# A fused two-block kernel on Trainium2: the late chunks of w_ada summed by one-column products

## What the kernel computes

```
mod = silu(c) @ w_ada + b_ada                 # 6 x 1024 columns, one row
shift_m, scale_m, gate_m, shift_f, scale_f, gate_f = split(mod, 6)
h = rms_norm(x, g_mix) * (1 + scale_m) + shift_m
proj = h @ w_in                               # 2896 columns: a, index and b heads
oa = attention over the 64 best keys by an index score (8 heads, top-k)
ob = attention with forget gates (8 heads, cumulative log f)
x = x + gate_m * (concat(rms_norm(oa), rms_norm(ob)) @ w_out)
h = rms_norm(x, g_ffn) * (1 + scale_f) + shift_f
x = x + gate_f * experts(h)                   # 32 experts, two chosen per token
```

## Time and profile before

| | before |
|---|---|
| median of 3 runs | 857.75 us (853.38 to 858.62) |
| the profiled execution | 857.29 us |
| its span, first to last instruction | 855.0 us |
| mean granted TensorE clock | 0.977 |
| PE / DVE / ACT / POOL busy | 809.1 / 297.6 / 170.5 / 60.2 us |

### The profile page before, as it was taken

One profiled execution on the slowest core, in us unless ns is written; L12 is line 12 of the kernel. 1 busy time (PEld: TensorE's weight loads), 2 busy tenths in 40 slices (PEclk: granted clock), 3 DMA queues, 4 the chain that ended last, 5 costly groups with the idle time before them and its releaser, 6 DMA issues.

```text
span 855.0 us, 9875 instructions
## 1 busy us (share of the span) xinstructions
PE 809.1 (95%) x3903; PEld 574.4 (67%) x3903; DVE 297.6 (35%) x674; ACT 170.5 (20%) x359; POOL 60.2 (7%) x55
## 2 busy tenths in 40 slices
PE   5889997899799999999999999999999999999996
PEld 3558775787335454444445786788888888888885
DVE  4278887654422121211212676344221111110004
ACT  4112322443411111010111337122210000000001
POOL 2243552000010000000000000000000000000000
PEclk9989998999899999999999999999999999999998
DMA  9988675436159999999998942214534442444001
GB/s 360 366 260 292 255 266 200 153 146 256 41 221 419 419 415 419 417 418 420 415 420 322 373 146 98 91 62 143 182 115 149 156 164 64 160 160 180 1 0 50
DMA packets 68188, 196.57 MB, mean 230 GB/s; under 512 B 2895, under 2 KB 30904, under 8 KB 59960
## 3 DMA queue, kind: packets, MB, share of 16 engines
q1 hardware_dynamic: 67344, 195.37, 60.3%
q0 software_dynamic: 288, 0.41, 0.2%
q10 hardware_dynamic: 520, 0.28, 0.1%
HBM read 194.80 MB, written 1.05 MB: 229 GB/s over the span
## 4 chain that ended last, share of the span: by engine, by line
PE 77%; DMA 14%; DVE 6%; issue 1%; SPq 1%; ACT 0%; DVEq 0%
PE ps L1327 18%; DMA ring<-in_w_down 10%; PE ps L1344 9%; PE ps L1066 8%; PE ps L640 8%; PE ps L1094 4%; PE ps L1087 4%; PE ps L765 4%; DMA ring<-in_w_ada 3%; PE ps L989 3%; DVE tok L1813 3%; PE ps L774 2%; PE ps L1053 2%; PE ps L961 2%; PE ps L951 2%; PE ps L1197 2%
## 5 line engine op out<-in xcount | busy, mean ns | idle before, releaser
L1327 PE MATMUL ps<-hT,ring 128*128 128x256 f32 x704 | 152.3, 379 | 0.9 <-DVE xT L2327 0.9
L1327 PEld LDWEIGHTS ps<-hT,ring 128*128 128x128 f32 x704 | 133.7, 190 | 19.4 <-issue 1.3
L1066 PE MATMUL ps<-ring,arena 128*64 128x512 f32 x512 | 113.2, 594 | 3.2 <-DMA ring<-in_w_down 3.2
L1066 PEld LDWEIGHTS ps<-ring,arena 128*64 128x64 f32 x512 | 38.8, 137 | 76.8 <-issue 70.8
L1344 PE MATMUL ps<-arena,ring 128*128 128x256 f32 x352 | 76.5, 379 | 0.3 <-PE ps L1327 0.3
L1344 PEld LDWEIGHTS ps<-arena,ring 128*128 128x128 f32 x352 | 66.6, 190 | 9.6 <-issue 0.7
L765 PE MATMUL ps<-hT,ring 128*128 128x256 f32 (+1 forms) x288 | 68.0, 391 | 0.9 <-ACT hT L1428 0.9
L765 PEld LDWEIGHTS ps<-hT,ring 128*128 128x128 f32 (+1 forms) x288 | 54.1, 192 | 14.3 <-issue 6.0
L1094 PE MATMUL ps<-arena 128*128 128x256 f32 x256 | 62.0, 386 | 0.9 <-DVE arena L2127 0.9
L1087 PE MATMUL ps<-ring,arena 128*64 128x512 f32 x256 | 58.5, 598 | 0.7 <-ACT arena L1610 0.7
L1094 PEld LDWEIGHTS ps<-arena 128*128 128x128 f32 x256 | 46.1, 190 | 18.9 <-issue 12.2
(11 more groups left out here) (396 smaller groups left out, 861.2 us busy)
## 6 DMA issues: line engine op xcount, KB each, us to landing
ring<-in_w_gate SPq DMA_DIRECT2D x32, 1024.0 KB, 10.2
ring<-in_w_up SPq DMA_DIRECT2D x32, 1024.0 KB, 12.2
ring<-in_w_down SPq DMA_DIRECT2D x32, 1024.0 KB, 12.7
ring<-in_w_gate_up SPq DMA_DIRECT2D x14, 1536.0 KB, 10.2
ring<-in_w_ada SPq DMA_DIRECT2D x5, 3072.0 KB, 10.8
ring<-in_w_in SPq DMA_DIRECT2D x9, 1024.0 KB, 14.6
ring<-in_w_down SPq DMA_DIRECT2D x3, 3072.0 KB, 10.2
ring<-in_w_ada SPq DMA_DIRECT2D x16, 512.0 KB, 11.5
```

What stands on the lines that cost most here:

```text
L1066: last = pe.matmul(ps[WIN * h:WIN * (h + 1), 0, :].rearrange("p (g n) -> p g n", g=2), lhsT=xw[:, u, k, WIN * h:WIN * (h + 1)], rhs=gu_w[: ...
L1327: last = pe.matmul(ps[:, t % 4, half * L:(half + 1) * L], lhsT=w[:, k, at:at + P], rhs=hT[:, k, :], start=k == 0, stop=k == KT - 1)
```

## The change

The row in between is gone. The one step `ada_cols(c)` does the sum over partitions and the turn at once: for each 128 columns of the chunk, the [128 x 128] piece is the stationary operand and a column of ones the one moving column, once for GpSimd's array and once for VectorE's. That is 12 products a chunk, 4 for the last. It stands where `ada_cols` stood, one projection later than `ada_rows` did, and it now signals `ada_rows_done`. `ada_done` is left for the extra work of chunks 3 and 4. `take_row` is gone from ScalarE.

```
-            def ada_rows(c):
+            def ada_cols(c):
-                w, n = weights("ada", c, KT, ada_width(c)), ada_width(c) // 2
-                chunk_there("ada", c)
+                w, n, at = weights("ada", c, KT, ada_width(c)), ada_width(c) // P, ada_columns(c)[0]
                 if c:
-                    pe.wait_ge(row_taken, c + 2)
                     pe.wait_ge(mod_ready, c + 2)
                 pe.wait_ge(ada_pool_ready, c + 1)
                 pe.wait_ge(ada_part_ready, c + 3)
-                for i, part in enumerate((w[:, DVE_K, :], ada_part(c))):
-                    for half in range(2):
-                        cols = slice(half * n, half * n + n)
-                        last = pe.matmul(ps[64 * half:64 * half + 64, 7, 0:n], lhsT=ones[:, 0:64], rhs=part[:, cols],
-                                         start=i == 0, stop=i == 1)
+                for i in range(n):
+                    for j, part in enumerate((w[:, DVE_K, :], ada_part(c))):
+                        last = pe.matmul(ps[:, 7, at.start + i:at.start + i + 1], lhsT=part[:, i * P:(i + 1) * P],
+                                         rhs=ones[:, 0:1], start=j == 0, stop=j == 1)
                 last.then_inc(ada_rows_done, 1)
```

TensorE's order at the start, and its six places in the attention pipeline (one of them is shown):

```
             dots(3, 1)
-            ada_rows(0)
-            pe.wait_ge(tile_taken, 5)
-            dots(0, 2)
...
             tokens(1, 260, 260, (0,), 252)
+            pe.wait_ge(tile_taken, 5)
+            dots(0, 2)
+            tokens(1, 260, 260, (1,), 252)
             dots(1, 3)
             ada_cols(0)
-            tokens(1, 260, 260, (1,), 252)
...
             features(2, 256 + P)
-            ada_rows(1)
             features(2, P)
             ada_cols(1)
```

ScalarE follows TensorE's new order (`relu_dots(0, 2)` after the first `take_values`, `relu_dots(1, 3)` after the second), and in pair 5 it takes `qA[2]` before `group_std(0, 1)`:

```
             softmax(5)
+            take(qA[:, 2, :], whole, SCALE)
             group_std(0, 1)
-            take(qA[:, 2, :], whole, SCALE)
```

VectorE copies `iwT` first, does three of the five steps of chunk 0, two score steps, the other two steps of chunk 0, and then the other six score steps. The forget-gate steps come after rounds 0 and 2 of the top-k in place of 3 and 6. In the pipeline the order of the last two is turned about, and `add_bias` has another wait:

```
+            ada_steps(0, range(0, 3))
...
+                if i == 1:
+                    ada_steps(0, range(3, DVE_K))
...
-                if r == 3:
+                if r == 0:
...
-                if r == 6:
+                if r == 2:
...
                 scale_probs(p)
-                add_bias(p + 1) if p < 4 else None
                 if p < 4:
                     ada_steps(p + 2)
+                    add_bias(p + 1)
...
-                ve.wait_ge(ada_done, c + 3)
+                ve.wait_ge(ada_rows_done, c + 3)
+                if c in (3, 4):
+                    ve.wait_ge(ada_done, c)
```

More of the change, by code:

```diff
@@ L262, in build @@
         row0 = cut(5888, 2, 512)
-        row = tokf[:, 1536:1920]
         both_halves = ident[:, 0:P:64]
@@ L722, in ada_rows @@
                 pe.wait_ge(ada_part_ready, c + 3)
-                for i, part in enumerate((w[:, DVE_K, :], ada_part(c))):
-                    for half in range(2):
-                        cols = slice(half * n, half * n + n)
-                        last = pe.matmul(ps[64 * half:64 * half + 64, 7, 0:n], lhsT=ones[:, 0:64], rhs=part[:, cols],
-                                         start=i == 0, stop=i == 1)
-                last.then_inc(ada_rows_done, 1)
[L730 to L736, removed]
+                for i in range(n):
+                    for j, part in enumerate((w[:, DVE_K, :], ada_part(c))):
+                        last = pe.matmul(ps[:, 7, at.start + i:at.start + i + 1], lhsT=part[:, i * P:(i + 1) * P],
+                                         rhs=ones[:, 0:1], start=j == 0, stop=j == 1)
+                last.then_inc(ada_rows_done, 1)
                 if c == 3:
@@ L743, in ada_cols @@
                                          start=k == 0, stop=k == KT - 1)
+                    last.then_inc(ada_done, 1)
                 if c == 4:
@@ L747, in ada_cols @@
                                      start=True, stop=True)
-                last.then_inc(ada_done, 1)
+                    last.then_inc(ada_done, 1)
             unit = Count()
@@ L900, in _ @@
             values(0)
-            ada_rows(2)
             features(3, 0)
@@ L908, in _ @@
             values(1)
-            ada_rows(3)
             features(3, P)
@@ L917, in _ @@
             values(2)
-            ada_rows(4)
             features(4, 0)
@@ L926, in _ @@
             values(3)
-            ada_rows(5)
             features(4, P)
@@ L1450, in relu_dots @@
                     act.activation(relu[:, half, :], ps[:, 2 + half, 0:NK], ACT.Relu).then_inc(dots_taken, 1)
-            def take_row(c):
-                act.wait_ge(ada_rows_done, c + 3)
-                act.activation(row[:, 0:ada_width(c) // 2], ps[:, 7, 0:ada_width(c) // 2], ACT.Copy).then_inc(row_taken, 1)
             take(kI[0:72, :], lambda o: o[0:72, 0:L])
@@ L1470, in _ @@
             relu_dots(3, 1)
-            take_row(0)
-            relu_dots(0, 2)
             def take_values(b, half):
@@ L1484, in _ @@
             take_values(0, 1)
+            relu_dots(0, 2)
+            take_values(1, 1)
             relu_dots(1, 3)
-            take_values(1, 1)
             take_values(0, 0)
@@ L1538, in _ @@
                     mixed(p - 1)
-                take_row(p + 1)
                 take(qB[:, p + 1, :] if p < 3 else qA[:, 0, :], whole, SCALE)
@@ L1544, in _ @@
             mixed(3)
-            take_row(5)
             take(qA[:, 1, :], whole, SCALE)
@@ L1802, in _, with ada_steps @@
                                  ALU.add).then_inc(h0_v, 1)
-            def ada_steps(c):
+            def ada_steps(c, tiles=range(DVE_K)):
                 w, part = weights("ada", c, KT, ada_width(c)), ada_part(c)
[L1807 to L1811, removed]
+                if tiles[0] == 0:
+                    ve.wait_ge(arrived[SLOT["ada", c]], ARRIVED["ada", c])
+                    if c >= 2:
+                        ve.wait_ge(ada_rows_done, c + 1)
+                    ve.tensor_scalar(part, w[:, 0, :], silu_c[:, 0:1], None, ALU.mult).then_inc(dve_step, 1)
+                for k in tiles:
+                    if k == 0:
+                        continue
                     own()
@@ L1840, in add_bias @@
                                  ).then_inc(mod_ready, 1)
-            ada_steps(0)
             ve.wait_ge(par_tr, 2)
```

## The result

| | before | after |
|---|---|---|
| median of 4 runs, beside each other on one chip | 856.05 us (853.38 to 858.62) | 867.11 us (863.78 to 868.08) |
| ratio, 95% interval | | 1.0119 [1.0081, 1.0156] |
| the profiled execution: time, span | 857.29, 855.0 us | 866.58, 864.3 us |

The changed kernel is slower by 11 us, more than the 1% that a measurement here can tell. The profiled executions differ by 9.3 us. Repeated on another chip in five rounds, it was 866.31 against 855.31 us, ratio 1.0132 [1.0093, 1.017].

What follows compares the result with a forecast made beforehand. The prediction took TensorE's chain to bound the kernel, with changes by 172 us carried to the end one to one. 857.29 + 5.5 (2.9 + 2.3 + 0.25) - 2.8 = 860.0 us; 8-in-10 range 853 to 866.

Steps and rivals of the forecast that it cites:

- the likeliest case: Whole kernel: early gain used up by later loads, `logits_of(4)` late, clock falls, end gains 2.8 us; 860.0 us, chance 0.45.
- The slowest rival: GpSimd's product of chunk 4 begins before `scale_probs(2)`'s second half; `logits(3)` +6.0 us, in all 863; chance 0.22.
- TensorE's own work: Chunk sums on TensorE: 24 passes take 2.3 to 3.0 us, taken as 2.6; +0.6 us a full chunk, +0.25 the last.
- chunk 3 is asked for at 95.0: Middle: the later, longer sum of chunk 1 puts chunk 3's load request at 95.0 us, against 93.1 before.
- chunk 4 at 122.4: Middle: with the DMA engines filled in the same order, chunk 4 lands at 122.4 us, 1.9 us later than before.
- I take it that it just gets through: Middle: `scale_probs(2)`'s second half begins at 122.5 us, as GpSimd begins chunk 4, and is not held.
- the stand in the top-k: Start: VectorE waits 2.4 us in the top-k for the forget gates' Ln, after the third `tokens` ends near 68.2.
- The second rival: Same as the slowest rival: GpSimd's product of chunk 4 holds VectorE's scaling 4 us more; 863 us, chance 0.22.
- The hold of the mask: Before `logits_of(0)`: chunk 1's GpSimd work falls under VectorE's mask and holds it, +1.4 us; start gains 3.0, not 4.7.
- the third rival: The waits vanish with nothing behind them, 14.2 us gained, 843; argued against by full bus and fixed swap latency; chance 0.03.
- The low clock behind the stand: TensorE stands from 141.7 to 148.1 before `logits_of(4)`; its clock then falls and costs 2.3 us.
- The end of the stretch: At `logits_of(6)`: taking the tile before `group_std` removes the 1.84 us wait and keeps the clock up; 2.8 us gained.

Runs made afterwards that it cites:

- e6: The changed kernel with 128 columns of ones as moving operand in place of one; 861.56 us, ratio 1.007 to the kernel before.
- e7: The changed kernel with SyncE holding the load of `w_out` until both halves of the `kA` swap have landed; 862.82 us, ratio 1.0088 to the kernel before.
- e2: The changed kernel with the one-step sums of chunks 1 to 5 back ahead of the projection; 860.93 us, ratio 1.0051 to the kernel before.
- e3: As e2 (sums early), with `add_bias` ahead of `ada_steps` again; 859.6 us, ratio 1.0049 to the kernel before.
- e4: The changed kernel, sums at their late places, with `add_bias` ahead of `ada_steps` again; 861.8 us, ratio 1.007 to the kernel before.
- e11: The changed kernel with the edits of e2, e3, e6 and e7, and log f after round 6; 856.94 us, ratio 1.0023 to the kernel before.
- e12: The kernel before with only `add_bias` moved behind `ada_steps`; 856.15 us, ratio 1.0005 to the kernel before.
- e5: The changed kernel itself, timed again in five rounds on another chip; 866.31 us, ratio 1.0132 to the kernel before.
- e9: The kernel before with `qA[2]` taken ahead of `group_std` and `w_out` held till the swap has landed; 852.62 us, ratio 0.9965 to the kernel before.
- e8: The changed kernel with GpSimd's product of chunk 4 held until `scale_probs(2)` is done; 864.97 us, ratio 1.0118 to the kernel before.
- e1: The new start alone, chunk 0 summed in one step, chunks 1 to 5 in two steps as before; 859.4 us, ratio 1.0029 to the kernel before.

## Why the prediction was wrong

The forecast was 860.0 in a range up to 866; it was 867.11. The direction of the likeliest case was right (slower), its size was about a quarter of it (2.7 of 11 us). The slowest rival, with 0.22, stood at 863; no case with a price lay above the range.

The profiles, term by term, in us against the kernel before:

| | forecast | measured |
|---|---|---|
| `logits_of(4)` starts later | +2.9 | +6.2 |
| from there to `logits_of(5)`, the low clock | +2.3 | +1.9 |
| from there to the out products | +0.25 - 2.8 | -1.5 |
| behind the out products | 0 | +2.7 |
| in all | +2.7 | +9.3 |

**TensorE's own work: right.** 24 passes in 2.6 to 2.8 us, and no wait at 52.

**The step that failed** is the first of these terms: "chunk 3 is asked for at 95.0", "chunk 4 at 122.4" and "I take it that it just gets through", with nothing put down for TensorE's clock behind the new sums. The relations held: from the request to chunk 4's product 27.3 us, walked as 27.4. The starting point was off by 3.5 us, 98.51 for 95.0. Of that, 2.2 us lie before `logits_of(0)` (85.58 for 83.4) and 1.3 between it and the request (12.9 for 11.6, a term whose own parts, 6.7, 3.65 and 1.16, give 11.5). Behind the 2.2 is the stand in the top-k, 4.41 us where I had 2.4: the third `tokens` ended at 71.2, not 68.2. Of these three microseconds 1.7 are the third `tokens` itself (5.32 us), at the low clock of 66 us, and 1.2 were there when the sum began (63.15, walked as 62): a fall of the clock at 32 to 36 us, in code that the change doesn't touch, had brought TensorE 1.6 us late to line 778 at 47.9 (46.35 before). With the 1.3 goes the low clock at 87 us, behind a stand; e6, where the clock stayed up, has 11.4 us there. My walk had the clock fall in one place, behind the stand for the swap, and allowed for none of these.

e6 shows it for the sums. With 128 columns the third `tokens` takes 3.52 us, the stand in the top-k is 2.73 us, and the rest comes out near the walk: `logits_of(0)` 84.02 (83.4 walked), chunk 3 asked for at 95.4 (95.0), chunk 4's product 122.58 (122.4), `logits_of(4)` 148.45 (148.1). The kernel is 4.8 us faster than the changed one. Part of the agreement is luck, since the clock also stayed up at 87 us there, which the columns don't decide, and since e6 has the fall at 32 us and the meeting, which the walk had not.

**The second rival took place, at a lower price.** GpSimd's product and the scaling met, by 0.01 us. Its deciding point was named rightly; its result, 863, rested on +3.1 us over the forecast. The traces put the meeting at 0.7 to 0.9 us. VectorE is held by GpSimd either way, only in another instruction. The hold of the mask, walked as 1.4 us, was there: its second half took 2.11 us with GpSimd at work and 0.63 before, though its first (line 1868, 0.36 us) was not held. The rule of the Trainium skill that the prediction drew on ("SBUF — State Buffer", section "Who interferes with whom") speaks of such exclusion for the whole instruction; the traces agree (4.49 for 0.62 us, 4.38 for 0.55), and the top-k's steps under GpSimd's product at 76.25 kept their time (0.76 us for three at 75.55, before it, and at 76.98, under it). In all `logits(3)` came at 140.49: +6.96, of which 5.3 are chunk 4's landing (1.9 walked) and 1.7 the meeting (nothing walked) and the bias (0.95 walked).

**The swap: the size of the hidden price.** I took its 6.9 us of landing as its latency, "fixed". With nothing ahead it is 2.0 to 2.1 us; the rest is `w_out`. It is in both kernels, so it did not make the difference between them, but the argument against the third rival, "the swap's latency is fixed", falls, and a gain was to be had: 3.5 us in the changed kernel by e7.

**The low clock behind the stand** was right in kind and near in size, though the stand itself was 3.84 us and not 6.4: from `logits_of(4)` to `logits_of(5)` 12.25 us against 10.34, +1.9 for 2.3, with 0.50 granted at 152.

**The end of the stretch: half right.** `logits_of(6)` has no wait. From `logits_of(5)` to the out products it is 15.12 us after and 16.59 before: 1.5 us gained, not 2.8 less 0.25. "Its reader has 5 us" overlooked that VectorE works off `group_std`'s readers ahead of `logits(6)`, for which TensorE now waits 2.33 us.

**Where the 11 us went,** by what each mending returns in the medians: the one-column passes' clock 4.8 (e6) and `w_out` ahead of the swap 3.5 (e7), each against the changed kernel on the same chip; the sums' later place some 7 by e2, which is across two chips and has the swap ahead of the load as well, but 2.2 by e3 against e4; the start 3.8 by itself, which has the low clock behind chunk 0's sum and the meeting in it; the meeting 0.7 to 0.9 in the traces. They can't be added, since several act on the same wait; e11 mends most of them together and returns 9. The order of the bias has 0.8 to 1.0 us of `logits(3)` and nothing that e12 can measure; the 5 us of e4 are, as far as its trace tells, those of the swap.

**What stays open.** The fall of the clock at 32 to 36 us is in 8 of the 11 profiled executions with the new start and in none of the 3 without it, though the instructions there are the same ones. It could be chance or not; it costs 1.6 us. The 1.7 us near 587 us are in the profiles of e5 and e9 too, and not in that of e6, so they don't hang on this change alone. The clock also falls differently from kernel to kernel: in e4, e7 and e8 behind the sums of chunks 0 to 3, in the changed kernel behind those of 0, 3 and 4. And how the 7 us of e2 divide into requests, swap and clock isn't told apart: its clock fell at 64 to 68 us as well.

## What to carry to other kernels

When a semaphore also releases loads, follow it to the queue before its signal is moved: here five sums moved by one projection (3.65 us), and chunk 4's product, 27 us behind the first request, came 3.4 to 3.7 us later for that alone, counted from `logits_of(0)` (e5 against e2, e4 against e3). A wait that is taken off TensorE can be worth nothing while another engine or a load sets the next meeting, as in e1; look first at what the same change asks for later. Put a small transfer that an engine waits for ahead of a big load, even if that holds the load back.

## What the runs showed of the hardware

- TensorE's clock fell to the lower of its levels while the engine was busy all through, 2.00 of 2.00 us, within or just behind 24 passes that move one column past 128 x 128 weights: behind three sums of five in the changed kernel, four of five in e4, e7 and e8. With 128 columns, at 2.88 us a sum for 2.77, it fell behind waits only, and the kernel is 4.8 us faster.
- The second of two copies of 64 KB on ScalarE's queue landed in 2.0 to 2.1 us where it was issued ahead of a load of 4 MB on SyncE's queue, by as little as 0.3 us, and in 5.9 to 7.4 us where the load's first 2 MB had been issued 0.1 us or more ahead of it.
- Two engines that shut each other out cost little more when they meet at another instruction: the 3.8 us that a scaling lost to GpSimd's product added 0.7 to 0.9 us to the whole row of steps up to `logits(3)`.
